# Gated delta rule in a two-block kernel: the keys' second turning dropped, the scalings and copies re-ordered

## The reference

```python
def gdn_branch(h, w_in, conv_w, a_log, dt_bias, norm_w, w_out):
    proj = h @ w_in                       # 1024 -> 4096 + 16
    qkv = silu(causal_depthwise_conv(proj[..., :3 * W], conv_w)); z = proj[..., 3 * W:4 * W]
    q = l2_normalize(q); k = l2_normalize(k)          # 8 heads of 128
    g = -exp(a_log) * softplus(a + dt_bias); beta = sigmoid(bt)
    o = chunk_gated_delta_rule(q, k, v, g, beta)
    o = o * rsqrt(mean(o * o) + RMS_EPS) * norm_w * silu(z)
    return o @ w_out

def chunk_gated_delta_rule(q, k, v, g, beta):
    g_cum = cumsum(g)                                  # inside a chunk
    lmat = (k * beta) @ k.T * decay_strict             # then (lmat + I) is inverted
    sol = triangular_solve(lmat + I, [v * beta, k * beta * exp(g_cum)])
    u, w = sol[..., :Dv], sol[..., Dv:]
    a_qk = q @ k.T * decay_incl
    for each chunk:
        v_new = u - w @ state
        o = (q * exp(g)) @ state + a_qk @ v_new
        k_dec = k * exp(g_last - g)
        state = state * exp(g_last) + k_dec.T @ v_new
```

## Time and profile before

| what | value |
|---|---|
| time, median of 3 runs | 841.61 us (840.64 to 842.58) |
| profiled execution: its time | 840.53 us |
| profiled execution: its span (first to last instruction) | 838.7 us |
| PE busy | 818.4 us, 98% of the span |
| DVE busy | 615.3 us, 73% |
| ACT busy | 487.8 us, 58% |
| GpSimd (POOL) busy | 68.2 us, 8% |
| mean granted TensorE clock | 0.998 |

### The profile page before, as it was taken

How to read it: one execution, slowest core, us unless ns; L and a number is a source line. 1 busy time by engine, 2 the same in 40 slices (tenths; PEclk the granted TensorE clock), 3 DMA queues, 4 the chain that set the end, 5 groups by cost and what they waited for, 6 DMA issues and landing times.

```text
span 838.7 us, 17644 instructions
## 1 busy us (share of the span) xinstructions
PE 818.4 (98%) x6596; PEld 764.3 (91%) x6596; DVE 615.3 (73%) x1053; ACT 487.8 (58%) x901; POOL 68.2 (8%) x72
## 2 busy tenths in 40 slices
PE   6999999999999999999999999999999999999997
PEld 3899988999999998989898888999999999999885
DVE  4498866768889766977877779664777996788543
ACT  3454565467689655584666457575556544555444
POOL 1000002400001002223100011000002120000000
PEclk9999999999999999999999999999999999999999
DMA  9999964804552221534644426434545454544521
GB/s 373 387 373 403 365 241 149 337 1 151 187 174 91 102 103 52 172 138 173 222 154 148 152 79 223 151 124 141 189 176 201 160 192 151 200 168 182 201 101 50
DMA packets 22012, 153.85 MB, mean 183 GB/s; under 512 B 2496, under 2 KB 2752, under 8 KB 3904
## 3 DMA queue, kind: packets, MB, share of 16 engines
q1 hardware_dynamic: 20592, 145.69, 47.4%
q0 software_dynamic: 1360, 7.34, 2.3%
HBM read 151.97 MB, written 1.05 MB: 182 GB/s over the span
## 4 chain that ended last, share of the span: by engine, by line
PE 86%; DVE 6%; ACT 3%; DMA 3%; issue 1%; SPq 0%; DVEq 0%
PE ps L402 46%; PE ps L1269 7%; PE ps L505 6%; PE ps L475 4%; PE ps L436 2%; DVE w_lo L1960 2%; PE ps L445 1%; PE ps L467 1%; ACT w_hi L1309 1%; PE ps L842 1%; DMA raw<-in_moba_first 1%; DMA proj<-in_ada_first 1%; PE ps L579 1%; PE ps L602 1%; DMA memkv<-in_ada_first 1%
## 5 line engine op out<-in xcount | busy, mean ns | idle before, releaser
L1960 DVE TENSOR_TENSOR w_lo<-raw,w_hi 128x1024 fp32r<-128x1024 f32 x230 | 285.8, 1248 | 96.4 <-ACT w_hi L1309 95.1
L1309 ACT CAST w_hi<-raw 128x1024 fp32r<-128x1024 f32 (+1 forms) x230 | 239.8, 1050 | 166.3 <-PE ps L402 65.1
L402 PE MATMUL ps<-in_hi,w_hi 128*128 128x256 f32 x1120 | 160.8, 286 | 1.7 <-issue 1.7
L402 PE MATMUL ps<-in_lo,w_hi 128*128 128x256 f32 x1120 | 157.2, 283 | 0.0
L402 PE MATMUL ps<-in_hi,w_lo 128*128 128x256 f32 x1120 | 157.2, 283 | 0.0
L402 PEld LDWEIGHTS ps<-in_hi,w_hi 128*128 128x128 f32 x1120 | 144.3, 191 | 6.2 <-issue 5.1
L402 PEld LDWEIGHTS ps<-in_hi,w_lo 128*128 128x128 f32 x1120 | 144.5, 192 | 0.0
L402 PEld LDWEIGHTS ps<-in_lo,w_hi 128*128 128x128 f32 x1120 | 144.4, 192 | 0.0
L2225 DVE SCALAR_TENSOR_TENSOR proj<-work,params,proj 128x256 f32 (+1 forms) x72 | 35.7, 496 | 8.0 <-ACT proj L1529 1.9
L2037 DVE SCALAR_TENSOR_TENSOR work<-raw,cs,work 128x1024 f32 x24 | 30.8, 1285 | 4.8 <-DVE w_lo L1960 2.0
L1269 PE MATMUL ps<-w_hi,in_hi 128*128 128x512 f32 x88 | 34.2, 389 | 0.0
(11 more groups left out here) (444 smaller groups left out, 1351.6 us busy)
## 6 DMA issues: line engine op xcount, KB each, us to landing
raw<-in_mixed SPq DMA_DIRECT2D x24, 1024.0 KB, 7.0
raw<-in_ffn_up SPq DMA_DIRECT2D x22, 1024.0 KB, 4.8
raw<-in_gdn_in SPq DMA_DIRECT2D x16, 1024.0 KB, 4.8
raw<-in_w_in SPq DMA_DIRECT2D x16, 1024.0 KB, 4.8
raw<-in_merge SPq DMA_DIRECT2D x12, 1024.0 KB, 4.8
raw<-in_ffn_down SPq DMA_DIRECT2D x11, 1024.0 KB, 4.8
raw<-in_branch SPq DMA_DIRECT2D x6, 1024.0 KB, 4.7
raw<-in_moba_out SPq DMA_DIRECT2D x4, 1024.0 KB, 7.0
```

Source lines behind the costliest of these rows:

```text
L402: mm = pe.matmul(half(u, 0), w[:, u, k * P:(k + 1) * P], a[:, base + k, :], start=(n == 0 and k == 0), stop=(n == 2 and k == UNIT - 1))
L1309: act.copy(w_hi[:, u, :], src).then_inc(hi_done, 1)
L1960: dve.tensor_tensor(w_lo[:, u, :], src, w_hi[:, u, :].bitcast(F32), ALU.subtract).then_inc(lo_done, 1)
```

## The change

On PE, `natural_k_again` goes. `natural_k(g)` for g = 2 and 3 waits for the scaled keys `gdn_kdg` of group g-2, since `decayed_k` now reads the first turning. z25 moves ahead of `natural_k(2)`, and z27 ahead of `natural_v`. On ACT, the decayed keys of groups 0 and 1 come behind their lengths, and those of groups 2 and 3 behind the copy of unit 25. The copies of z24 and z25 are parted from their `high`. On POOL, the clearing of `tt` goes, and the two `kcol` operations come from DVE. The scatter into `tt` is one transpose on DVE, then one masked multiplication on DVE and one on ACT.

```diff
-                pe.wait_ge(*after("gdn_length", g - 1))
+                pe.wait_ge(*after("gdn_kdg", 4 * (g - 1)))
...
         z_unit(24)
+        z_unit(25)
         natural_k(2)
         natural_k(3)
-        z_unit(25)
         for g in range(4):
             gram_k(g)
         z_unit(26)
         pe.wait_ge(*after("gdn_lt", 4))
-        pe.wait_ge(*after("gdn_length", 4))
+        pe.wait_ge(*after("gdn_kdg", 12))
...
+        z_unit(27)
         for g in range(4):
             natural_v(g)
-        z_unit(27)
-        natural_k_again(0)
-        natural_k_again(1)
         z_unit(28)
-        natural_k_again(2)
-        natural_k_again(3)
         z_unit(29)
...
-        pe.wait_ge(*after("gdn_scattered", 4))
+        pe.wait_ge(*after("gdn_scattered", 3))
...
         for g in range(4):
             decay_q(g)
-        for g in range(4):
+        act.wait_ge(*after("gdn_kx", 2))
+        link(act.activation(kcol[:, 0, :], kcol[:, 0, :], ACT.Exp))
+        for g in range(2):
+            lengths(g)
+            decayed_k(g)
+        z_copy(24)
+        for g in (2, 3):
             lengths(g)
...
         for g in range(4):
             decay(g)
-        act.wait_ge(*after("gdn_kx", 2))
-        act.activation(kcol[:, 0, :], kcol[:, 0, :], ACT.Exp).then_inc(sem("gdn_root"), 1)
-        z_out(24)
+        high("gdn_in", 28)
+        z_copy(25)
+        for g in (2, 3):
+            decayed_k(g)
         for b in range(2):
             act.wait_ge(*after("conv_free", GROUP + 4 * (b + 5)))
             silu(16 + 4 * b)
-        z_out(25)
+        high("gdn_in", 29)
...
         z_out(27)
-        for g in range(4):
-            decayed_k(g)
         z_out(28)
         z_out(29)
+        act.wait_ge(*after("gdn_scattered", 1))
+        act.activation(tt[:, :, 32:64], turned, ACT.Copy, scale=parity(5)).then_inc(sem("gdn_scattered"), 1)
...
-        dve.tensor_tensor(kcol[:, 0, 0:8], gcol[:, 32:40], gcol[:, 0:8], ALU.subtract).then_inc(sem("gdn_kx"), 1)
-        dve.tensor_copy(kcol[:, 0, 8:16], gcol[:, 8:16]).then_inc(sem("gdn_kx"), 1)
...
-        for b in range(4):
-            r = slice(32 * b, 32 * b + 32)
-            dve.transpose(tt[r, :, 32 * (b % 2):32 * (b % 2) + 32].rearrange("p m (h c) -> p c h m", h=2),
-                          gathered[r].rearrange("p c (h m) -> p c h m", h=2)).then_inc(sem("gdn_scattered"), 1)
+        dve.transpose(turned.rearrange("p m (h c) -> p c h m", h=2),
+                      gathered[:].rearrange("p c (h m) -> p c h m", h=2)).then_inc(sem("gdn_scattered"), 1)
+        dve.wait_ge(*after("gdn_scattered", 1))
+        dve.tensor_scalar(tt[:, :, 0:32], turned, parity(4), None, ALU.mult).then_inc(sem("gdn_scattered"), 1)
...
-        pool.memset(tt, 0.0).then_inc(sem("gdn_zero"), 1)
...
+        pool.wait_ge(*after("gdn_col_done", 1))
+        pool.tensor_tensor(kcol[:, 0, 0:8], gcol[:, 32:40], gcol[:, 0:8], ALU.subtract).then_inc(sem("gdn_kx"), 1)
+        pool.tensor_copy(kcol[:, 0, 8:16], gcol[:, 8:16]).then_inc(sem("gdn_kx"), 1)
```

More of the change, by code:

```diff
@@ L102 @@
 CONSTS = [("ident", P), ("one", P), ("neg", 3 * P), ("back", 3 * P), ("upper", P), ("colmask", S),
-          ("pick", 31), ("parity", 4)]
+          ("pick", 31), ("parity", 6)]
 CCOL = {}
@@ L240, in _program @@
     middle = area(3344, 64, of=core_a)
+    turned = area(2560, MATS, 32, of=core_b)
     tc, tt = area(4096, MATS, C), area(1024, MATS, C, of=core_b)
@@ L1573, in lengths, with z_copy, z_out @@
             ins.then_inc(sem("gdn_length"), 1)
-        def z_out(n):
+        def z_copy(n):
             act.wait_ge(unit_done, FIRST["gdn_in"] + n + 1)
             act.copy(proj[:, n, :], half(n % 2 if n < 30 else 6, 0)).then_inc(taken, 1)
+        def z_out(n):
+            z_copy(n)
             if n < 28:
@@ L1600, in decayed_k @@
         def decayed_k(g):
-            act.wait_ge(*after("gdn_natk", 4 + g + 1))
             for j in range(4):
-                act.activation(kdg[:, 4 * g + j, :], ps[:, 2 + g, j * P:(j + 1) * P], ACT.Copy,
+                act.activation(kdg[:, 4 * g + j, :], ps[:, 2 + g % 2, j * P:(j + 1) * P], ACT.Copy,
                                scale=column(0, 4 * g + j)).then_inc(sem("gdn_kdg"), 1)
@@ L1632, in _ @@
         z_out(26)
-        act.wait_ge(*after("gdn_root", 3))
+        act.wait_ge(*after("gdn_root", 2))
         for g in range(4):
@@ L1660, in _ @@
             act.copy(pm[:, mats(s), :], blocks(s)).then_inc(sem("gdn_ps"), 1)
-        act.wait_ge(*after("gdn_scattered", 4))
+        act.wait_ge(*after("gdn_scattered", 3))
         for n in range(2):
@@ L2284, in _ @@
         low("gdn_in", 28)
-        dve.wait_ge(*after("gdn_zero", 4))
+        dve.wait_ge(*after("gdn_zero", 3))
         dve.wait_ge(*after("gdn_packed", 1))
@@ L2338, in _ @@
         link(dve.tensor_scalar(gathered[:, :, 16:32], square16(inverse), parity(3), None, ALU.mult))
-        dve.wait_ge(*after("gdn_zero", 2))
-        for b in range(4):
-            r = slice(32 * b, 32 * b + 32)
-            dve.transpose(tt[r, :, 32 * (b % 2):32 * (b % 2) + 32].rearrange("p m (h c) -> p c h m", h=2),
-                          gathered[r].rearrange("p c (h m) -> p c h m", h=2)).then_inc(sem("gdn_scattered"), 1)
+        dve.transpose(turned.rearrange("p m (h c) -> p c h m", h=2),
+                      gathered[:].rearrange("p c (h m) -> p c h m", h=2)).then_inc(sem("gdn_scattered"), 1)
+        dve.wait_ge(*after("gdn_scattered", 1))
+        dve.tensor_scalar(tt[:, :, 0:32], turned, parity(4), None, ALU.mult).then_inc(sem("gdn_scattered"), 1)
         def masked_q(g):
@@ L2707, in _ @@
         pool.memset(ct, 0.0).then_inc(sem("gdn_zero"), 1)
-        pool.memset(tt, 0.0).then_inc(sem("gdn_zero"), 1)
         pool.memset(inverse, 0.0).then_inc(sem("gdn_zero"), 1)
-        pool.wait_ge(*after("gdn_zero", 3))
+        pool.wait_ge(*after("gdn_zero", 2))
         pool.memset(inverse.rearrange("p (d s) -> p d s", s=17)[:, :, 0:1], 1.0).then_inc(sem("gdn_zero"), 1)
+        pool.wait_ge(*after("gdn_col_done", 1))
+        pool.tensor_tensor(kcol[:, 0, 0:8], gcol[:, 32:40], gcol[:, 0:8], ALU.subtract).then_inc(sem("gdn_kx"), 1)
+        pool.tensor_copy(kcol[:, 0, 8:16], gcol[:, 8:16]).then_inc(sem("gdn_kx"), 1)
         for g in range(4):
@@ L2748, in _constants @@
     even = np.where(np.arange(P) % 32 < 16, 1.0, 0.0)
+    first = np.where(np.arange(P) % 64 < 32, 1.0, 0.0)
     out = {
@@ L2756, in _constants @@
         "upper": np.where(j >= i, 0.0, NEG),
-        "parity": np.stack([-even, even - 1.0, even, 1.0 - even], 1),
+        "parity": np.stack([-even, even - 1.0, even, 1.0 - even, first, 1.0 - first], 1),
     }
```

## The result

The changed kernel takes 844.12 us in the median of 8 executions (842.30 to 846.04), against 841.20 (840.64 to 842.58) for the kernel before in 8. The ratio is 1.0036, with a 95% interval of 1.0026 to 1.0046: slower by 3.0 us (2.9 between the two medians). The forecast was 843.7, in a range of 842.2 to 845.1, and slower. One execution of the kernel before, in a later comparison, was in another, slow state (1340.91 us at a mean granted clock of 0.558) and counts in no number here.

What follows compares the result with a forecast made beforehand. PE's order plus its waits bound the kernel; waits of 1.6 and 2.5 us for ACT's copies put the turning of `tt` at 283.0 to 283.2 against 280.95. So 841.61 + 2.1 = 843.7 us, range 842.2 to 845.1.

Steps and rivals of the forecast that it cites:

- ACT's queue sets z28 and z29: ACT's copies of z26 and z27 come late behind the scaled keys, so PE waits 1.6 us at z28, 2.5 at z29.
- the same slots: PE's distances from one start to the next where nothing waits, such as 2.96 us for a z unit, 1.72 for the values.
- The chain of ACT's starts: ACT's queue followed start by start from 252.59: z28 can start at 272.8, z29 at 278.3; z27's copy 3.1 to 3.4 later.
- the two prices for a scaled key: On ACT: 0.25 us from the trace, used in the sum, or 0.29 from the skill, which would give +2.4.
- the rival of the faster queue: ACT's four `ct` copies take 1.1 us less, so time rises only 0.4 to 1.4, about 842.5; 22 in 100.
- `lt` isn't delayed: DVE's `lt` follows the first decay, ending at 261.2, so packing on PE was forecast some 0.3 us late.
- No wait at the turning of `tt`: The scatter's ACT half is ready at 282.5, PE arrives at 283.0; the earlier 0.63 us wait is gone.
- The note that ACT's half would be the last wait: If ACT were early, its half of `tt` would keep the turning of `tt` at z29's end + 1.3 us.
- The sum, +2.1: The turning of `tt` on PE comes at 283.0 to 283.2 against 280.95, so the kernel is 2.1 us slower.
- the clock, my rival at 4 in 100: Granted clock falls to 1.2 GHz in PE's two new pauses; z29 takes 2.96 us more, about 846.7; 4 in 100.
- PE's own saving: If PE never waited for ACT, the turning of `tt` would come at 278.75, 2.2 us earlier than before.

Runs made afterwards that it cites:

- the early copies: Changed kernel with ACT's copy of z27 ahead of the sixteen scaled values, then also z26's ahead of the silus; ratio to before 0.9995 each.
- the eight keys left out: Changed kernel without the eight scaled keys of groups 2 and 3 on ACT; ratio to before 1.0015.
- the filler: Changed kernel with filler matmuls on PE in its two new pauses, two in front of z28 and four in front of z29; ratio to before 1.0023.
- The load alone in before: Kernel before with sixteen more activations in ACT's queue, four behind each group of lengths, each the size of a scaled key; ratio 1.0028.
- the kernel with both copies early: Changed kernel with ACT's copies of z26 (ahead of the silus) and z27 (ahead of the scaled values) moved forward; ratio to before 0.9995.
- once no copy is late: Changed kernel with z26's and z27's copies moved forward and both masked halves of `tt` on DVE; 838.64 us, ratio to before 0.9973.
- The two kernels with one pause of 1.88 or 2.04: 1.88: changed kernel without eight scaled keys, ratio 1.0015. 2.04: z26's and z27's copies forward, scatter on DVE, z27 back behind the values, ratio 1.0011.

## Why the prediction was right, point by point

- **ACT's queue sets z28 and z29: right, and shown** by the early copies, by the eight keys left out and by the filler, with which the pauses stay where they were. The load alone in before makes the same loss, at other places. Forecast waits 1.6 and 2.5, measured 1.54 and 2.51 by the same slots (1.35 and 2.37 of idle time).
- **The chain of ACT's starts: 0.4 us too long.** Counted from z24, z29 was due at 278.3 - 250.96 = 27.34 and came at 26.97, and the copy of z27 came 2.76 later than before, not 3.1 to 3.4. PE was early by as much, so the waits came out right. Ln and the two Exp took 262.30 - 261.73 = 0.57, not 0.73 (there the first decay may have waited for `diff`), the linked Exp 0.26 instead of 0.35, and a decay 0.52 instead of 0.54. Of the two prices for a scaled key, the trace kept its 0.25; the Trainium skill's 0.29 (ScalarE: Activation LUTs, What ACT_TABLE_LOAD costs) isn't what these runs show.
- **The `ct` copies don't get faster.** 274.03 - 271.92 = 2.11 against 2.12: the rival of the faster queue is out.
- **`lt` isn't delayed.** I had it 0.3 us late behind the first decay. It starts 10.00 us after z24 (263.05 here), 9.98 before, and packing 14.28 against 14.26.
- **No wait at the turning of `tt`: right,** with z29 late. The note that ACT's half would be the last wait if ACT were early is what the kernel with both copies early met.
- **The sum, +2.1: right in its own terms, 0.3 too high.** Without the clock it is +1.78 (filler) or 3.31 - 1.36 - 0.13 = +1.82. The measured +3.0 lies outside of these terms: the clock, my rival at 4 in 100, priced 2.96 us in z29 alone. It happened, in both profiles of the changed kernel and by the mean clock in six of the first eight executions, and cost 1.36 and 1.28, under half of that price. This term was wrongly left out, and the range held the time by its upper half, which I had set for other reasons: that part is luck. The Trainium skill's warning (TensorE: Matmul & The Clock Gate, HAM oscillation) is of long idle gaps that take the clock down. The trace agrees that the clock goes down with idle time: 0.50 in the stretch behind the second pause. The gaps that the Trainium skill describes there, though, are longer than either of these two. I had set the fall aside because the trace of before shows none. But that trace has no such pauses, and the earlier trace rows couldn't have shown it: a slice is 21 us wide, and the changed kernel's row on the page of the profile, with the fall in it, has the same forty nines.
- **PE's own saving: right.** 2.2 us forecast, 2.37 measured once no copy is late.

What stays open is why the clock falls in some executions of the same kernel and not in others, behind a pause and in the small products alike. For the small products 6 of 49 against 2 of 89 hints that the new order makes the fall likelier, and is too little to show it.

## What to carry to other kernels

When a step moves to an earlier place in an engine's queue, write down everything it is moved past, the bank or buffer releases above all, and give each its new time: dropping 1.6 us of work from the busiest engine here cost 3 us, because 4 us of small operations now stood ahead of two copies of 0.4 us. The repair is to issue the release as soon as its data is there and put the long run behind it. Where a sum opens a pause on TensorE that the trace of before doesn't have, price the clock too, and look for its fall in stretches of 2 us and in the clock of every execution: one profile of the kernel without eight keys showed none, and six of its ten executions had one.

## What the runs showed that I had not expected

TensorE's granted clock fell to 1.2 GHz at the second of two pauses, 1.35 and 2.37 us, that lie 3 us of matmuls apart (4.32 and 4.24 us for a unit of 2.96). In the second profile it fell already inside the pause, 0.93 in the stretch from 276 to 278 us, where PE stands still. It stayed up in the same place with the pauses filled to 0.46 and 0.63. The two kernels with one pause of 1.88 or 2.04 show no fall in their one profile each, but a mean clock of 0.996 or less in six of ten and four of twelve executions (before: 2 of 89). With one pause of 1.34 it is one of eleven, and with pauses of 1.56 and 1.44 that start over eight us apart none of six.

The clock also fell for some 6 us with PE busy throughout, in products of 64x64 tiles and the 128x128 ones after them, which cost 3 us, in 3 of 13 profiles. And a DVE transpose of 128x512 costs 1.04 to 1.15 us in the ten profiles that have it, as much as one of 32x512 (1.1): the four of before did the work of one.

```profile
278.43 1.05 DVE L2332 STREAM_TRANSPOSE core_b<-core_b 128x512 f32<-128x512 f32 x1
```
